# Copying the expert gate and up weights into 16 KB runs per partition during attention

## The chip, the cores and the metric

The kernel runs on one core of a Trainium2 chip (trn2). The metric is the device time of one execution in microseconds; the kernel before has a median of 1999.08 us in 3 runs, from 1995.08 to 2000.13 us. Everything is computed in 32-bit floats. The engines are named as in the profile: PE (TensorE, the matmuls), PEld (its weight loads), DVE (VectorE), ACT (ScalarE), POOL (GpSimd) and SP (SyncE, which here only issues DMAs). SBUF is the memory on the core with 128 partitions, PSUM takes the matmul results, and DRAM is the memory outside.

## The reference

One layer of a streaming encoder over 2048 tokens of width 1024:

```
h = modulate(rms_norm(x), sh1, sc1);  proj = h @ w_in
attn = latent attention (8 heads, chunks of 64 tokens, block-causal)
conv = gated depthwise convolution of 3 taps
x = x + g1 * (concat(rms_norm(attn), rms_norm(conv)) @ w_out)
h2 = modulate(rms_norm(x), sh2, sc2)
x = x + g2 * hier_moe(h2)        # top group of 4, then top 2 of its 8 experts
return rms_norm(x, final_g)
```

The part that the change feeds is the mixture of experts. Each of the 32 experts is a small MLP, `(silu(h @ w_gate[e]) * (h @ w_up[e])) @ w_down[e]`, with `w_gate` and `w_up` of shape 32 x 1024 x 256 and `w_down` of 32 x 256 x 1024. So an expert has 1 MB each of gate, up and down weights, 96 MB in all.

## The kernel before

The program has six stages, each a function with a block of its own in which every engine has a list of work. A stage begins when all engines have left the one before. In the profiled execution they lie roughly so: `project` (0 to 440 us) computes the modulation and the input projection; `attend` (443 to 1060 us) the attention; `mix` (1060 to 1330 us) the output projection and the router's logits; `route` and the tables at the start of `experts` choose tokens (to 1378 us); `experts` runs to 1950 us; `combine` does the last norm.

**Attention.** PE, DVE, ACT and POOL work through 8 heads, in two Python-unrolled halves `b` inside 4 values of `hp` (a loop on SP, unrolled on the others). A head has 40 steps (`STEPS_HEAD`), and its queries go in 4 groups of 512 (`GROUPS`). When a group is complete, ACT copies the sums out of PSUM, DVE inverts them and POOL multiplies (`divide`, line 1207) into one of the two buffers `on`, and counts up `divided`. SP waits for that count and stores `on` to `mix_dram` with two DMAs of 64 KB (line 802), counting `stored[0]` or `stored[1]`. POOL's `divide` two groups later reuses the buffer and first waits for that store (`hold(po, stored[p], ...)`). The last thing that SP does in the stage is to wait until all stores have landed. In this stage SP issues nothing else but two small loads of constants at its start.

**Mixing.** Its first DMAs, issued by SP as soon as the block begins, are a tile of `mix_dram` (line 1300), `w_out` in 4 parts of 1 MB (line 1314), the late modulation sums (1297) and a tile of `x` (1303). ACT issues the router's weights (lines 1522 to 1527). ACT and DVE then split `w_out` into a high and a low part (1562, 1509) before PE can begin (1347).

**Experts.** A loop over 16 pairs of experts. For each expert `b` of a pair, POOL gathers up to 192 token rows from `xs_dram` by an indirect DMA (`xa`, `xb`, line 1792), PE turns them (1863, 1864, 1874), ACT and DVE copy them to `xTe`. `gate_up` multiplies them by the gate and up weights (PE, line 1886), ACT and DVE make the activation, `down_first` and `down_rest` multiply by the down weights (1894), and POOL adds the scaled result to `x2_dram` by an indirect, accumulating DMA (1796). The weights have two buffers each, `wg`, `wu` and `wd`, one for each expert of a pair. SP waits for `up_done`, which PE raises when it is through with the buffers, and issues the next gate and up loads (lines 1782, 1783), then waits for `dlo_ready` and issues the down load (1785). In DRAM a gate or up matrix is 1024 rows of 256 numbers, so that each piece of such a load is 1 KB; each partition takes 8 of them. PE waits for both with one count, 32 for an expert (`ld_gu`).

Of the kernel before, what the change touches and what calls it, by code (L numbers as in the profile page):

```python
# [8 lines left out]
P = 128  # L9
# [8 lines left out]
D = 1024  # L18
KD = D // P
S = 2048  # L20
# [16 lines left out]
NEXP = 32  # L37
NGRP = 4
EPG = NEXP // NGRP
FE = 256  # L40
KF = FE // P
CAP = 192
# [642 lines left out]
GROUPS = NT // GQ  # L685
# [38 lines left out]
def attend(nc, T, st):  # L724
# [5 lines left out]
    with ExitStack() as ctx:  # L730
        sb = lambda name, shape, dt=F32: ctx.enter_context(nc.sbuf_tensor(name, shape, dt))
        sem = lambda name: ctx.enter_context(nc.semaphore(name))
        cst, cols, cs, qn, kvn, KR, mix_dram = (st[k] for k in (
            "cst", "cols", "cs", "qn", "kvn", "KR", "mix_dram"))
        Qhi, Qlo = sb("Qhi", [P, 2, S], F32R), sb("Qlo", [P, 2, S], F32R)
        Khi, Klo = sb("Khi", [P, 2, S], F32R), sb("Klo", [P, 2, S], F32R)

# [22 lines left out]
        scores_done, out_done, out_free, divided = (sem(n) for n in (  # L760
            "scores_done", "out_done", "out_free", "divided"))
        stored = [sem("on_stored0"), sem("on_stored1")]
        dve_step, inverted, passed_pool = sem("dve_step2"), sem("inverted"), st["passed_pool"]
        block = ctx.enter_context(nc.Block())

        def key_cols(i, n):

            return min(512, (i + 1) * P - n * 512)
# [17 lines left out]
        @block.sync  # L786
        def _(sp):
            for k in range(2):
                sp.dma_start(qf[QKD:QKD + 1 + GQ, k], T["consts"][QKD:QKD + 1 + GQ, C_ROWS + k * 512:C_ROWS + (k + 1) * 512]
                             ).then_inc(ld_rows, 16)  # L790
            sp.sem_inc(stored[0], 32)
            sp.sem_inc(divided, 2)
            sp.sem_inc(plo_done, RING)

            for s in st["done_sems"]:
                sp.sem_clear(s)
            with sp.Fori(0, HEADS // 2) as hp:
                for b in range(2):
                    for g in range(GROUPS):
                        sp.wait_ge(divided, hp * 2 * GROUPS + (b * GROUPS + g + 4))  # L800
                        for h in range(2):
                            sp.dma_start(mix_dram[VD * b:VD * (b + 1), bass.ds(hp, 1),
                                                  g * 512 + h * 256:g * 512 + (h + 1) * 256],
                                         on[h * VD:(h + 1) * VD, (g + 1) % 2:(g + 1) % 2 + 1]
                                         ).then_inc(stored[(g + 1) % 2], 16)
            sp.wait_ge(stored[0], 32 * (HEADS * GROUPS // 2 + 1))
            sp.wait_ge(stored[1], 32 * HEADS * GROUPS // 2)

# [913 lines left out]
def experts(nc, T, st):  # L1722

    with ExitStack() as ctx:
        sb = lambda name, shape, dt=F32: ctx.enter_context(nc.sbuf_tensor(name, shape, dt))
        sem = lambda name: ctx.enter_context(nc.semaphore(name))
        cst, modc, rank, marks, rounds, xs_dram, x2_dram, g2row = (st[k] for k in (
            "cst", "modc", "rank", "marks", "rounds", "xs_dram", "x2_dram", "g2row"))
        PAIRS = NEXP // 2
        inslot = sb("inslot", [P, NT * 2, CAP], BF16)  # L1730

# [9 lines left out]

        xT = sb("xTe", [P, KD, 2 * CAP])
        cols_of = (slice(0, CAP), slice(CAP, 2 * CAP))
        wg, wu, wd = sb("wg", [P, 2, KD, FE]), sb("wu", [P, 2, KD, FE]), sb("wd", [P, 2, KF, D])
        sg, aT = sb("sg", [P, KF, CAP]), sb("aT", [P, KF, CAP])

        dhi, dlo = sb("dhi", [P, 2, KF, D], F32R), sb("dlo", [P, 2, KF, D], F32R)
# [3 lines left out]
        turn, gate, up, outa, outb = bank[:, 0:2], bank[:, 2], bank[:, 3], bank[:, 4:6], bank[0:CAPB, 6:8]  # L1751
# [5 lines left out]
        ld_gu, ld_wd = [sem("ld_gu0"), sem("ld_gu1")], [sem("ld_wd0"), sem("ld_wd1")]  # L1757
        gate_done, up_done, silu_done = sem("gate_done"), sem("up_done"), sem("silu_done5")
# [9 lines left out]
        def load_rounds(eng):  # L1768
            return eng.value_load(rounds[0:1, 0:1], min_val=1, max_val=ROUNDS)

        @block.sync
        def _(sp):
            n_rounds = load_rounds(sp)
            wgd = T["w_exp_gate"].rearrange("l e (k p) n -> p (l e k) n", p=P)
            wud = T["w_exp_up"].rearrange("l e (k p) n -> p (l e k) n", p=P)
            wdd = T["w_exp_down"].rearrange("l e (k p) n -> p (l e k) n", p=P)
            with sp.Fori(0, n_rounds) as r:
                with sp.Fori(0, PAIRS) as ep:
                    for b in range(2):

                        sp.wait_ge(up_done, r * NEXP + ep * 2 + (b + 1))
                        sp.dma_start(wg[:, b], wgd[:, bass.ds(ep * 2 * KD + b * KD, KD), :]).then_inc(ld_gu[b], 16)
                        sp.dma_start(wu[:, b], wud[:, bass.ds(ep * 2 * KD + b * KD, KD), :]).then_inc(ld_gu[b], 16)
                        sp.wait_ge(dlo_ready, r * NEXP + ep * 2 + (b + 1))
                        sp.dma_start(wd[:, b], wdd[:, bass.ds(ep * 2 * KF + b * KF, KF), :]).then_inc(ld_wd[b], 16)

# [62 lines left out]
        def _(pe):  # L1849
# [26 lines left out]

            def gate_up(q, b, r):

                pe.wait_ge(ld_gu[b], r * (PAIRS * 32) + q * 32 + 32)
                pe.wait_ge(turn_dve, r * (PAIRS * 3) + q * 3 + (3 + b))  # L1880
                pe.wait_ge(turn_act, r * (PAIRS * 3) + q * 3 + (3 + b))
                pe.wait_ge(mlp_step, r * (NEXP * 3) + q * 6 + (b * 3 + 1))
                for w, out, done in ((wg, gate, gate_done), (wu, up, up_done)):
                    for f in range(KF):
                        for k in range(KD):
                            ins = pe.matmul(out[:, f * CAP:(f + 1) * CAP], w[:, b, k, f * P:(f + 1) * P],  # L1886
                                            xT[:, k, cols_of[b]], start=k == 0, stop=k == KD - 1)
                    ins.then_inc(done, 1)

# [21 lines left out]
            with pe.Fori(0, n_rounds) as r:  # L1911
# [4 lines left out]
                for first, last, b, lo, at in ((0, P, 4, 0, tokens), (0, CAPB, 5, P, tokens), (CAPB, P, 5, P, tokens),  # L1916
                                               (0, P, 6, 0, others), (0, CAPB, 7, P, others)):
                    pe.wait_ge(slots_ready, r * 2 + (1 if b == 4 else 2))
                    for j in range(NT * 2):
                        ins = pe.matmul(bank[first:last, b, at], inslot[:, j, lo:lo + last - first],  # L1920
                                        marks[:, j // 2, j % 2, at], start=j == 0, stop=j == NT * 2 - 1)
# [267 lines left out]
def program(nc, T, out):  # L2189
    with ExitStack() as whole:  # L2190
        def tensor(scope, side=None):
            return lambda name, shape, dt=F32: scope.enter_context(nc.sbuf_tensor(name, shape, dt, side=side))

        keep = tensor(whole)
        scratch = lambda name, shape: nc.dram_tensor(name, shape, F32, kind="Internal").ap()
        st = {"done_sems": [], "cst": keep("cst", [P, C_SMALL]), "cols": keep("cols", [P, 96]), "modc": keep("modcol", [P, 32]),
              "csil": keep("csil", [P, KD]),
              "mod_dram": scratch("mod_dram", [P, LATE_HALVES, 512]), "g1row": keep("g1row", [P, D]), "g2row": keep("g2row", [P, D]), "fgrow": keep("fgrow", [P, D]),
              "mix_dram": scratch("mix_dram", [P, 2 * NCH, S]), "x2_dram": scratch("x2_dram", [S + 2 * CAP, D]),
              "xs_dram": scratch("xs_dram", [S, D])}  # L2200

        st["passed"], st["passed_pool"] = (whole.enter_context(nc.semaphore(n)) for n in ("passed", "passed_pool"))
        with ExitStack() as mixers:
            left = tensor(mixers)
            st["cs"] = left("cs", [P, S])
            st["wuq"] = left("wuq", [P, KQ, (HEADS + 1) * QKD])
            st["wuk"], st["wuv"] = left("wuk", [P, (HEADS + 1) * NOPE]), left("wuv", [P, (HEADS + 2) * VD])
            st["qn"], st["kvn"], st["KR"] = left("qn", [P, KQ, S]), left("kvn", [P, S]), left("KR", [P, S])
            project(nc, T, st)
            attend(nc, T, st)  # L2210
        st["logits"] = keep("logits", [P, NT, NGRP + NEXP])
        mix(nc, T, st)
        st["gates"], st["rank"] = keep("gates", [P, NT * 2]), keep("rank", [P, NT * 2])
        st["marks"], st["rounds"] = keep("marks", [P, NT, 2, MARKS * NEXP], BF16), keep("rounds", [P, 1], I32)
        route(nc, T, st)
        experts(nc, T, st)
        combine(nc, T, st, out)
# [20 lines left out]
```

## Time and profile before

| | us |
|---|---|
| median of 3 runs | 1999.08 |
| lowest and highest run | 1995.08, 2000.13 |
| span of the profiled execution | 1996.9 |
| PE busy in the span | 1804.3 (90%) |
| DVE, ACT, POOL busy | 1181.1, 854.9, 855.0 |
| bytes read from and written to DRAM | 229.13 MB, 60.82 MB |

The profile has one profiled execution. Its page gives busy times, the span in 40 slices of about 50 us (a digit is a busy share in tenths; 9 is 90% or more), the DMA queues, the costliest groups of instructions and the DMA issues. Behind the page stands the trace, which can be asked for windows of time, for waits and who ended them, and for the instructions in order. The DMA share is the mean over the core's 16 DMA engines; as packets overlap it can pass 1. PE's granted clock is given as a share of full speed. "Landing" is the time from the issue of a DMA to the arrival of its last byte.

### The profile page before, as it was taken

The page shows a single profiled execution, that of the slowest core. Times are in us where ns is not written, and L with a number is a line of the kernel's source. Part 1 is how long each engine was busy: PE and PEld are TensorE (multiplying, and loading weights), DVE is VectorE, ACT ScalarE, POOL GpSimd, SP SyncE. Part 2 cuts the span into 40 slices and gives each one's busy share as a digit, 9 for nine tenths or more (in the row PEclk, how much of TensorE's full clock was granted, in tenths as well). Part 3 has the DMA queues.
Part 4 walks back from the last instruction along what each step waited for, and adds up shares of the span by engine and source line. Part 5 has one row for each costly group of instructions (what it writes and reads, how often), then busy time and mean ns, then how long its engine had stood idle before and what let it go on. Part 6 is the DMA issues. An engine that isn't in the chain of part 4 may idle for free. (4 is left out here: it accounts for less than half of the span.)

```text
span 1996.9 us, 26921 instructions
## 1 busy us (share of the span) xinstructions
PE 1804.3 (90%) x8987; PEld 1482.5 (74%) x8988; DVE 1181.1 (59%) x2015; ACT 854.9 (43%) x1520; POOL 855.0 (43%) x887
## 2 busy tenths in 40 slices
PE   2999999997999999999995999965999999999970
PEld 2777878764777777777784788854999988888960
DVE  4687889956766766666645555553444444444434
ACT  3535454326777677667684132311222222222214
POOL 0132314103888888888892111122243434434330
PEclk9999999996999999999996999977999999999995
DMA  7656555530000000000006344415899998999948
GB/s 282 197 164 185 172 163 165 147 95 0 6 9 6 9 9 6 11 7 6 11 11 218 105 157 141 143 43 189 278 268 276 279 276 270 278 276 274 272 91 336
DMA packets 216176, 291.05 MB, mean 146 GB/s; under 512 B 24373, under 2 KB 172048, under 8 KB 215834
## 3 DMA queue, kind: packets, MB, share of 16 engines
q1 hardware_dynamic: 193498, 220.60, 33.3%
q0 software_dynamic: 20224, 69.22, 13.9%
q8 instruction: 43, 0.70, 0.1%
q10 hardware_dynamic: 2368, 0.17, 0.1%
q14 instruction: 43, 0.35, 0.1%
HBM read 229.13 MB, written 60.82 MB: 145 GB/s over the span
## 5 line engine op out<-in xcount | busy, mean ns | idle before, releaser
L1212 POOL TENSOR_TENSOR plo<-KR,phi 128x512 fp32r<-128x512 f32 (+1 forms) x320 | 352.3, 1118 | 44.8 <-ACT KR L1171 44.6
L1020 DVE TENSOR_REDUCE cmax<-tbank 128x1 f32<-128x512 f32 (+2 forms) x320 | 193.4, 605 | 106.4 <-PE tbank L835 101.2
L1170 ACT ACTIVATE phi<-tbank 128x512 fp32r<-128x512 f32 (+1 forms) x320 | 170.7, 533 | 141.6 <-PE tbank L884 137.1
L387 PE MATMUL pbank<-hhi,wslhi 128*128 128x512 f32 x512 | 207.9, 406 | 6.7 <-DVE wsllo L440 6.7
L1946 DVE TENSOR_SCALAR xTe<-ebank,modcol 128x256 f32<-128x256 f32 (+1 forms) x128 | 53.7, 472 | 258.9 <-PE ebank L1864 137.6
L387 PE MATMUL pbank<-hhi,wsllo 128*128 128x512 f32 x512 | 201.9, 394 | 0.0
L387 PE MATMUL pbank<-hlo,wslhi 128*128 128x512 f32 x512 | 201.9, 394 | 0.0
L331 POOL DMA_DIRECT2D wmod<-in_w_ada x64 | 48.4, 757 | 305.2 <-DVE macc L519 295.2
L1886 PE MATMUL ebank<-xTe,wg 128*128 128x192 f32 x1024 | 171.8, 326 | 3.1 <-DVE ahi L1974 1.8
L1886 PEld LDWEIGHTS ebank<-xTe,wg 128*128 128x128 f32 x1024 | 167.9, 190 | 7.9 <-DVE ahi L1974 2.1
L1886 PE MATMUL ebank<-xTe,wu 128*128 128x192 f32 x1024 | 171.6, 326 | 0.0
L1171 ACT ACTIVATE KR<-tbank 128x512 f32<-128x512 f32 (+1 forms) x320 | 169.2, 529 | 0.0
L1886 PEld LDWEIGHTS ebank<-xTe,wu 128*128 128x128 f32 x1024 | 167.3, 190 | 0.0
L2080 ACT ACTIVATE xTe<-ebank,modcol 128x256 f32<-128x256 f32 (+1 forms) x128 | 56.7, 508 | 233.9 <-PE ebank L1864 147.1
L925 PE MATMUL tbank<-phi,VVhi 128*128 128x512 f32 (+1 forms) x320 | 134.7, 421 | 3.8 <-ACT phi L1170 3.7
L835 PE MATMUL tbank<-Khi,Qhi 96*128 96x512 f32 (+2 forms) x320 | 122.0, 384 | 5.4 <-DVE cmax L1020 5.1
L1573 POOL TENSOR_TENSOR mlo<-mixed,mhi 128x1024 fp32r<-128x1024 f32 x16 | 38.3, 2394 | 200.9 <-ACT mhi L1533 200.9
L387 PEld LDWEIGHTS pbank<-hhi,wslhi 128*128 128x128 f32 x512 | 97.7, 191 | 30.0 <-DVE wsllo L440 7.8
L883 PE MATMUL tbank<-Qhi,Klo 96*128 96x512 f32 (+1 forms) x320 | 118.2, 370 | 0.0
L903 PE MATMUL tbank<-plo,VVhi 128*128 128x512 f32 (+1 forms) x322 | 117.8, 366 | 0.3 <-POOL plo L1212 0.2
L884 PE MATMUL tbank<-Qlo,Khi 96*128 96x512 f32 (+1 forms) x320 | 117.9, 368 | 0.0
L926 PE MATMUL tbank<-phi,VVlo 128*128 128x512 f32 (+1 forms) x320 | 117.3, 367 | 0.0
(283 smaller groups left out, 3976.8 us busy)
## 6 DMA issues: line engine op xcount, KB each, us to landing
wg<-in_w_exp_gate SPq DMA_DIRECT2D x32, 1024.0 KB, 5.9
wu<-in_w_exp_up SPq DMA_DIRECT2D x32, 1024.0 KB, 9.0
wd<-in_w_exp_down SPq DMA_DIRECT2D x32, 1024.0 KB, 7.6
wraw<-in_w_in SPq DMA_DIRECT2D x60, 512.0 KB, 4.2
wmod<-in_w_ada POOLq DMA_DIRECT2D x64, 256.0 KB, 3.4
xt<-in_x SPq DMA_DIRECT2D x4, 2048.0 KB, 12.7
wada<-in_w_ada SPq DMA_DIRECT2D x4, 2048.0 KB, 18.7
mixed<-mix_dram SPq DMA_DIRECT2D x16, 512.0 KB, 4.3
```

The source lines that it names most:

```text
L387: ins = pe.matmul(out, w[:, S % 3, k], h[:, n % 2, k], start=k == 0 and j == 0, stop=k == KD - 1 and j == 2)
L835: pe.matmul(plain[:, chunk % 2, 0:w], Qhi[0:QKD, b, i * P:(i + 1) * P], Khi[0:QKD, b, n * 512:n * 512 + w], start=True, stop=True).then_in ...
L883: pe.matmul(out, Klo[0:QKD, b, k], Qhi[0:QKD, b, q], start=False, stop=False)
L884: pe.matmul(out, Khi[0:QKD, b, k], Qlo[0:QKD, b, q], start=False, stop=True).then_inc(scores_done, 1)
L903: ins = pe.matmul(outp[:, g % 2, first_tile(g, kt) * P:512], heads_values(VVhi, kt, b), step_of(plo, m), start=False, stop=last)
L925: pe.matmul(out, heads_values(VVhi, kt, b), step_of(phi, m), start=kt == 0, stop=False)
L926: pe.matmul(out, heads_values(VVlo, kt, b), step_of(phi, m), start=False, stop=False)
L1020: W(ve.tensor_reduce(cmax[:, i % 2, n:n + 1], plain[:, chunk % 2, 0:w], AX.X, ALU.max), plain_read)
L1170: A(act.activation(step_of(phi, m), scores[:, m % 2, j * P:512], ACT.Exp), phi_done)
L1171: A(act.activation(step_of(probs, m), scores[:, m % 2, j * P:512], ACT.Exp), exp_done)
L1212: po.tensor_tensor(step_of(plo, m), step_of(probs, m), step_of(phi, m).bitcast(F32), ALU.subtract).then_inc(plo_done, 1)
L1886: ins = pe.matmul(out[:, f * CAP:(f + 1) * CAP], w[:, b, k, f * P:(f + 1) * P], xT[:, k, cols_of[b]], start=k == 0, stop=k == KD - 1)
```

## The change

A new scratch tensor in DRAM, `wgu_dram`, holds for each expert and partition one run of 16 KB: 8 KB of gate weights and then 8 KB of up weights, in the order in which the partition takes them. During attention, each time that SP has issued the two stores of a group, it issues two copies of 1 MB from `w_exp_gate` and `w_exp_up` to `wgu_dram`, DRAM to DRAM, for one expert (`copy_expert`). With 8 heads of 4 groups that makes the 32 experts. At the end of the stage SP waits until all 64 copies have landed, ahead of its waits for the stores. In the experts, the buffers `wg` and `wu` become one, `wgu`, of the same size; one DMA of 2 MB takes the place of the two of 1 MB, and PE waits for 16 in place of 32.

```diff
+            def copy_expert(hp, j):
+                for n, name in enumerate(("w_exp_gate", "w_exp_up")):
+                    src = T[name].rearrange("l e (k p) n -> p (l e k) n", p=P)
+                    sp.dma_start(wgu_rows[:, bass.ds(hp * 2 * GROUPS + j, 1), n * KD:(n + 1) * KD],
+                                 src[:, bass.ds(hp * 2 * GROUPS * KD + j * KD, KD)].rearrange(
+                                     "p (e k) n -> p e k n", e=1)).then_inc(expert_copied, 16)
+
             with sp.Fori(0, HEADS // 2) as hp:
                 for b in range(2):
                     for g in range(GROUPS):
...
                                          ).then_inc(stored[(g + 1) % 2], 16)
+                        copy_expert(hp, b * GROUPS + g)
+            sp.wait_ge(expert_copied, 16 * 2 * NEXP)
             sp.wait_ge(stored[0], 32 * (HEADS * GROUPS // 2 + 1))
...
-        wg, wu, wd = sb("wg", [P, 2, KD, FE]), sb("wu", [P, 2, KD, FE]), sb("wd", [P, 2, KF, D])
+        wgu, wd = sb("wgu", [P, 2, 2 * KD, FE]), sb("wd", [P, 2, KF, D])
...
-            wgd = T["w_exp_gate"].rearrange("l e (k p) n -> p (l e k) n", p=P)
-            wud = T["w_exp_up"].rearrange("l e (k p) n -> p (l e k) n", p=P)
+            wgud = wgu_dram.rearrange("(e p) k n -> p e (k n)", p=P)
...
-                        sp.dma_start(wg[:, b], wgd[:, bass.ds(ep * 2 * KD + b * KD, KD), :]).then_inc(ld_gu[b], 16)
-                        sp.dma_start(wu[:, b], wud[:, bass.ds(ep * 2 * KD + b * KD, KD), :]).then_inc(ld_gu[b], 16)
+                        sp.dma_start(wgu[:, b:b + 1].rearrange("p e k n -> p e (k n)"), wgud[:, bass.ds(ep * 2 + b, 1)]
+                                     ).then_inc(ld_gu[b], 16)
...
-                pe.wait_ge(ld_gu[b], r * (PAIRS * 32) + q * 32 + 32)
+                pe.wait_ge(ld_gu[b], r * (PAIRS * 16) + q * 16 + 16)
...
-                for w, out, done in ((wg, gate, gate_done), (wu, up, up_done)):
+                for lo, out, done in ((0, gate, gate_done), (KD, up, up_done)):
...
-                            ins = pe.matmul(out[:, f * CAP:(f + 1) * CAP], w[:, b, k, f * P:(f + 1) * P],
+                            ins = pe.matmul(out[:, f * CAP:(f + 1) * CAP], wgu[:, b, lo + k, f * P:(f + 1) * P],
```

## Rows read from the trace of the kernel before

**Rows 1.** Page: busy us, 40 slices in tenths, matmul groups (busy us, mean ns | idle)

```profile
PE 1804.3 (90%) x8987; PEld 1482.5 (74%) x8988; DVE 1181.1 (59%) x2015; ACT 854.9 (43%) x1520; POOL 855.0 (43%) x887
...
PE   2999999997999999999995999965999999999970
...
DMA  7656555530000000000006344415899998999948
...
L1886 PE MATMUL ebank<-xTe,wg 128*128 128x192 f32 x1024 | 171.8, 326 | 3.1 <-DVE ahi L1974 1.8
...
L1886 PE MATMUL ebank<-xTe,wu 128*128 128x192 f32 x1024 | 171.6, 326 | 0.0
```

**Rows 2.** Windows by stage: length, busy per engine (instructions), PE clock, DMA share, GB/s

```profile
400.00:1050.00 650.00, 628.16 (x2755) 472.87 (x2754) 409.85 (x862) 436.68 (x909) 486.79 (x515) 0.97 0.05 14
...
1350.00:1950.00 600.00, 563.14 (x3360) 507.62 (x3360) 261.75 (x349) 132.64 (x194) 220.37 (x227) 0.97 0.86 252
```

**Rows 3.** The same view, one pair of experts of the loop

```profile
1657.00:1692.00 35.00, 35.00 (x205) 31.66 (x204) 16.09 (x21) 8.13 (x12) 14.54 (x16) 1.00 0.94 271
```

**Rows 4.** Waits in the experts: engine, line <- releaser: total us, times, longest

```profile
PE ebank L1863 <- DMA xb<-xs_dram,ib: 9.3, 1, 9.3
```

**Rows 5.** Waits of the SP queue in the experts, same columns

```profile
SPq L1782 <- PE ebank L1886: 203.2, 30, 28.2
```

**Rows 6.** DMA issues by line: count, KB each, median us to landing

```profile
wg<-in_w_exp_gate SPq DMA_DIRECT2D x32, 1024.0 KB, 5.9
wu<-in_w_exp_up SPq DMA_DIRECT2D x32, 1024.0 KB, 9.0
...
mix_dram<-on SPq DMA_DIRECT2D x64, 64.0 KB, 1.9
```

**Rows 7.** Timeline where attention ends: start us, length us, engine, operation [idle before]

```profile
1057.64 1.13 SPq L802 DMA_DIRECT2D mix_dram<-on  x2
1060.65 0.66 SPq L1300 DMA_DIRECT2D mixed<-mix_dram  x1
...
1060.65 0.46 ACTq L1522 DMA_DIRECT2D wr<-in_w_router_group  x1
...
1071.92 1.19 PE L1347 MATMUL mbank<-whi,mhi 128*128 128x512 f32 x2 [18.72 <-DVE wlo L1509]
```

**Rows 8.** Timeline of POOL: the divides that release the stores

```profile
521.78 0.73 POOL L1207 TENSOR_TENSOR on<-raw,rs 128x256 f32<-128x256 f32 x1
...
1013.03 0.74 POOL L1207 TENSOR_TENSOR on<-raw,rs 128x256 f32<-128x256 f32 x1
...
1030.69 0.74 POOL L1207 TENSOR_TENSOR on<-raw,rs 128x256 f32<-128x256 f32 x1
...
1045.01 0.74 POOL L1207 TENSOR_TENSOR on<-raw,rs 128x256 f32<-128x256 f32 x1
...
1056.76 0.72 POOL L1207 TENSOR_TENSOR on<-raw,rs 128x256 f32<-128x256 f32 x1 [3.94 <-DVE rs L1037]
```

**Rows 9.** Windows: first expert weights; last scatters (1942:1946); final stage

```profile
1358.00:1362.00 4.00, 2.17 (x37) 2.02 (x38) 3.84 (x3) 0.00 (x0) 0.00 (x0) 0.50 1.09 361
1362.00:1366.00 4.00, 4.00 (x78) 3.94 (x76) 1.09 (x6) 0.00 (x0) 0.00 (x0) 0.59 1.05 388
...
1942.00:1944.00 2.00, 0.00 (x0) 0.00 (x0) 0.00 (x0) 0.00 (x0) 0.20 (x1) 0.50 0.98 180
1944.00:1946.00 2.00, 0.00 (x0) 0.00 (x0) 0.00 (x0) 0.00 (x0) 0.00 (x0) 0.50 0.83 160
...
1965.00:1970.00 5.00, 0.00 (x0) 0.00 (x0) 2.01 (x6) 3.29 (x8) 0.00 (x0) 0.50 1.03 410
```

**Rows 10.** Timeline at the experts' start, and landing of the xb gathers

```profile
1368.92 0.96 POOL L1792 DMA_INDIRECT xb<-xs_dram,ib  x1 [0.30 <-issue]
...
1378.32 0.47 PE L1863 MATMUL ebank<-cst,xa 128*128 128x128 f32 x1 [9.30 <-DMA xb<-xs_dram,ib]
...
DMA to landing us min/median/max: 5.0/5.4/9.2
```

More of the change, by code:

```diff
@@ L732, in attend @@
         sem = lambda name: ctx.enter_context(nc.semaphore(name))
-        cst, cols, cs, qn, kvn, KR, mix_dram = (st[k] for k in (
-            "cst", "cols", "cs", "qn", "kvn", "KR", "mix_dram"))
+        cst, cols, cs, qn, kvn, KR, mix_dram, wgu_dram = (st[k] for k in (
+            "cst", "cols", "cs", "qn", "kvn", "KR", "mix_dram", "wgu_dram"))
         Qhi, Qlo = sb("Qhi", [P, 2, S], F32R), sb("Qlo", [P, 2, S], F32R)
@@ L762, in attend @@
         stored = [sem("on_stored0"), sem("on_stored1")]
+        expert_copied = sem("expert_copied")
         dve_step, inverted, passed_pool = sem("dve_step2"), sem("inverted"), st["passed_pool"]
         block = ctx.enter_context(nc.Block())
+        wgu_rows = wgu_dram.rearrange("(e p) k n -> p e k n", p=P)
         def key_cols(i, n):
@@ L1726, in experts @@
         sem = lambda name: ctx.enter_context(nc.semaphore(name))
-        cst, modc, rank, marks, rounds, xs_dram, x2_dram, g2row = (st[k] for k in (
-            "cst", "modc", "rank", "marks", "rounds", "xs_dram", "x2_dram", "g2row"))
+        cst, modc, rank, marks, rounds, xs_dram, x2_dram, g2row, wgu_dram = (st[k] for k in (
+            "cst", "modc", "rank", "marks", "rounds", "xs_dram", "x2_dram", "g2row", "wgu_dram"))
         PAIRS = NEXP // 2
@@ L2199, in program @@
               "mix_dram": scratch("mix_dram", [P, 2 * NCH, S]), "x2_dram": scratch("x2_dram", [S + 2 * CAP, D]),
-              "xs_dram": scratch("xs_dram", [S, D])}
+              "xs_dram": scratch("xs_dram", [S, D]),
+              "wgu_dram": scratch("wgu_dram", [NEXP * P, 2 * KD, FE])}
         st["passed"], st["passed_pool"] = (whole.enter_context(nc.semaphore(n)) for n in ("passed", "passed_pool"))
```

## The prediction, made before the changed kernel was run

> **What bounds the kernel now.** I read the page first. TensorE (PE) is busy for 90% of the span, and the PE line of the 40 slices stays at 9 except where one stage hands over to the next; the DMA line is at 8 or 9 over the last third, the experts, and at 0 over the attention [rows 1]. Those two lines invite the change, so the question is whether the busy DMA engines of the experts hold anything up. The table of windows by stage says how much there could be: attention (400 to 1050 us) has DMA at 0.05, the experts (1350 to 1950 us) have DMA at 0.86 and PE 563.14 of 600 us [rows 2]. The 36.86 us without PE are not in the loop: a window of about one pair of experts, 35 us, has PE busy for 35.00 us at clock 1.00, with DMA at 0.94 beside it [rows 3]. The waits of that stage agree. Only one wait of PE on a DMA is there, 9.3 us, once, for the first gathered rows [rows 4]. None is for wg or wu. The wait runs the other way: the SP queue, which issues the weights, stood 203.2 us in 30 waits for PE to free a buffer [rows 5]. A 1 MB weight transfer lands in 5.9 us (gate) or 9.0 us (up, queued behind it) [rows 6]. Its buffer is free for a pair's 35 us less the gate and up matmuls of one expert, (171.8 + 171.6) / 32 = 10.7 us [rows 1]: 24 us. So the loop is bound by PE and the weights are hidden, with 15 us to spare.
>
> The other place that matters is the end of attention, where the new work ends. The last two stores are issued from 1057.64 us, 1.13 us for both; the mixing stage's first DMAs start at 1060.65 us on the SP and ACT queues at the same instant, so a barrier lets them go, and it waits for the store to land, 1.9 us [rows 6, 7]. From there to the first matmul of the mixing stage at 1071.92 us everything is a chain of loads and splits with no cover: PE stood for 18.72 us [rows 7].
>
> **The change, part by part.** *Expert loads.* Two 1 MB issues per expert become one of 2 MB, with 16 KB runs. In the loop it removes waits of nobody. Even if it took 2 or 3 us off each landing, PE would still have 0 us to win; if 16 KB runs were somehow slower, the 15 us of slack cover that. I enter 0; it would cost from a landing above 24 us on. The SP queue issues one DMA less per expert, 32 in all, at about 0.5 us; SP waits for PE anyway [rows 5], so 0.
>
> *Start of the experts.* Here loads and gathers do meet. The gather of xb is issued at 1368.92 us and PE starts on it at 1378.32 us, 9.4 us later, while its landings have a median of 5.4 us [rows 10]. It is behind what is left of the first 6.3 MB of weights. The engines move these at 361 and 388 GB/s with 1 KB gate and up rows; the last stage, all rows of 4 KB, reaches 410 [rows 9]. If 16 KB runs brought the 4.2 MB of gate and up from 375 to 410 GB/s, they would end 11.2 - 10.2 = 1.0 us sooner. Bounds: 0 and, if the gather were wholly freed, 9.4 - 5.4 = 4.0 us. I take 0.5 us gained, since the other transfers stay.
>
> *The copies in attention.* 32 pairs of 1 MB copies, DRAM to DRAM, 1 KB pieces, 67.1 MB. They touch no SBUF, and the engines of attention wait for no loads. The DMA share there is 0.05 [rows 2], so the room is there. Each pair is issued on SP behind the two stores of a group. The store that follows is queued behind it, and POOL's divide, two groups later, waits for that store. Where divides come closest, in the last head, two of them span 1030.69 - 1013.03 = 17.7 us [rows 8]; a store behind one pair is in time as long as T + 1.9 is less than that. That part is 0.
>
> *The last copy.* This is the term that counts. The last pair is issued right behind the last store, and the new wait on expert_copied stands ahead of the barrier. Queued behind that wait are all DMAs of the mixing stage, and all five engines. Nothing hides it. Its cost is one issue between the last store and the first copy (0.5 us, about half of the 1.13 us [rows 7]) plus the transfer time T of 2.10 MB; the fixed 1.9 us to land is paid already by the store.
>
> T has no row: no transfer of the kernel before goes from DRAM to DRAM. Above, a copy cannot beat a plain load or store, 410 GB/s in the last stage where both directions mix [rows 9]: T = 5.1 us. The nearest row from below is the accumulating scatter, which reads DRAM and writes it back within one packet: with nothing else in flight it moved 180 and 160 GB/s (counted once) at engine shares 0.98 and 0.83 [rows 9], so 184 to 193 GB/s at full share: T = 11.4 us. If an engine's read and write side share the 410 GB/s of the mixed row, a copy gets 205 GB/s: T = 10.2 us; with the loss of 1 KB rows (375 against 410) it is 187 GB/s and T = 11.2 us. These last three agree and I take 190 GB/s, T = 11.0 us.
>
> The Trainium skill (DMA: Bandwidth & Descriptors, Latency and other measured facts) gives 207 to 214 GB/s per direction for copies between HBM tensors with 16 KiB rows and slower ones where the pitch between partitions is 512 KiB or more; here it is 16 KB and 1 KB. By it T would be an estimated 10.0 us and the sum 1 us lower; no row of before shows such a copy.
>
> *Backlog.* Is the queue empty when the last pair is issued? The last five divides are at 1013.03 us, one between, 1030.69, 1045.01 and 1056.76 us [rows 8], each sending one pair some 2 us later (1056.76 us for the last, its stores from 1057.64 us and 1.13 us long), so the five have moved by 1015 + 5T or by 1058.8 + T, whichever is later, and land 1.9 us behind. The two cross at T = 11.0 us. So at 11.0 there is no backlog yet, but no margin either: each us of T beyond it costs 5 us. In the earlier heads a pair has 18.2 us on average: the divide at 1013.03 us is the 27th after the one at 521.78 us, which lets the first pair go [rows 8].
>
> **The sum.** 0.5 + 11.0 - 0.5 = +11.0 us on the profiled execution: span 1996.9 to 2007.9 us. The median of the runs, 1999.08 us, stands 2.2 us above the span, as start and end outside it; so 2010.1 us.
>
> **Rivals.** (1) *Backlog*: the copy runs at 140 to 170 GB/s, because each 1 KB piece costs the engines more between two DRAM addresses than the scatter's 4 KB pieces. T = 13.5 us: the five pairs end at 1015 + 67.5 + 1.9 = 1084.4 instead of 1060.3 us, +24 us, less 0.5: 2022.7. For it speaks that the scatter's row was taken with 4 KB pieces; against it that loads with 1 KB pieces lose only 9%. It decides from T = 11.0 us.
> (2) *Fast copy*: read and write overlap fully, T = 5.1 to 7 us, +5.6 to +7.5, less 0.5: 2005. The scatter speaks against it, though its addition may be what slows it.
> (3) *Not slower*: the same fast copy, +5.6 us, and the first gather finds an empty queue, -4.0 us: 2000.7. With the whole 4.0 us gained, it decides from T below 9.5 us (0.5 + 9.5 - 4.0 = 6.0 us, 0.3%). Against it: the DMA engines are full at 1.09 and 1.05 while the first weights load [rows 9], so bytes, not runs, set the end. For a time well below 1999 I find no idle time of PE that the change could remove beyond the 9.3 us [rows 4].
> (4) *Copies that don't fit*: below 115 GB/s (2.1 MB in 18.2 us) the queue grows through all of attention. At 100 GB/s, T = 21: 523 + 32 x 21 = 1195 us instead of 1060, +135 us: 2134. The stores would also hold POOL's divides. Nothing in the trace points so low.
>
> **How the numbers follow.** Forecast (T of 9 to 11.5 us, 2008 to 2013) 0.52; backlog 0.24; fast copy 0.12; not slower 0.07; doesn't fit 0.05. A measurement of this kernel can tell about 0.3% (6 us) from no change, 1993.1 to 2005.1. The fast copy straddles the bound with half of its chance, so same gets 0.06 + 0.06 = 0.12; faster 0.03, from a gain at the start of the experts that I have no row for; slower 0.85. The range leaves out part of rival 3 below and rival 4 and the slow end of rival 1 above: 2003 to 2028.
>
> **What would show it.** In the profile after: DMA share in attention about 0.6 (11.0 of 18.2 us) where it was 0.05; PE in attention unchanged at 628 us of 650; the first DMA of the mixing stage 11 us later behind the last store, and PE's wait before its first matmul near 30 us where it was 18.72; the expert loop still about 35 us a pair with PE full, whatever the landing of wgu. The landing of the copies tells T: with the second of a pair above some 13 us the backlog is there. Wrong would be: a wait of PE or POOL in attention on a store or on its own instructions, a pair of experts that gets shorter, or a handover that is not longer than before.

## The result

The changed kernel takes 2005.21 us (median of 10 runs, 2001.75 to 2007.38), the kernel before 1998.83 us in the same series (10 runs). The medians differ by 6.4 us, 0.32%. The ratio on record, which is not the quotient of these two medians, is 1.0039, with a 95% interval from 1.0027 to 1.0050: slower by 5.4 to 10.0 us. The profiled execution has a span of 2002.6 us where it was 1996.9 us, +5.7. The forecast was 2010.1 us, +11.0.

The page after the change: span, busy times, PE and DMA over the 40 slices, and the DMA issues that are new (count, KB each, median us to landing).

```profile
span 2002.6 us, 27098 instructions
...
PE 1802.1 (90%) x8988; PEld 1479.4 (74%) x8988; DVE 1181.2 (59%) x2015; ACT 855.3 (43%) x1520; POOL 858.2 (43%) x887
...
PE   2899999997999999999994999965999999999970
...
DMA  7656555520233442432547344414889889989848
...
wgu<-wgu_dram SPq DMA_DIRECT2D x32, 2048.0 KB, 8.5
wgu_dram<-in_w_exp_gate SPq DMA_DIRECT2D x32, 1024.0 KB, 6.1
wgu_dram<-in_w_exp_up SPq DMA_DIRECT2D x32, 1024.0 KB, 7.5
```

PE and the other engines are as busy as before [rows 1]. Where the DMA line stood at 0 during attention it now has 2 to 5, and the largest part of the longer span is the handover to the mixing stage, as shown below. The windows by stage (length, busy time per engine with instructions, PE clock, DMA share, GB/s):

```profile
400.00:1050.00 650.00, 627.94 (x2742) 472.00 (x2741) 409.31 (x861) 435.17 (x905) 484.74 (x512) 0.97 0.34 110
...
1350.00:1950.00 600.00, 568.29 (x3392) 511.18 (x3390) 267.61 (x361) 132.99 (x195) 228.86 (x231) 0.97 0.82 251
```

In attention PE is busy for 627.94 us of 650, before 628.16, with the DMA engines at 0.34 instead of 0.05 [rows 2]. In the experts the DMA share fell from 0.86 to 0.82 at the same 251 GB/s, with the same bytes in longer runs, and PE is as busy as it was in the loop (the window of the table is fixed, and the stage now begins later in it).

The end of attention is the place. The timeline of the SP queue there, and PE's first matmul of the mixing stage (start us, length us):

```profile
1059.75 1.24 SPq L812 DMA_DIRECT2D mix_dram<-on  x2
1061.28 0.64 SPq L803 DMA_DIRECT2D wgu_dram<-in_w_exp_gate  x1
1062.18 0.64 SPq L803 DMA_DIRECT2D wgu_dram<-in_w_exp_up  x1
1069.99 0.64 SPq L1312 DMA_DIRECT2D mixed<-mix_dram  x1
...
1081.36 1.19 PE L1359 MATMUL mbank<-whi,mhi 128*128 128x512 f32 x2 [26.07 <-DVE wlo L1521]
```

The stretch from the issue of the last stores to the first load of the next stage is called the handover below. It took 1060.65 - 1057.64 = 3.0 us [rows 7] and takes 1069.99 - 1059.75 = 10.2 us: +7.2. Of these 10.2 us, 1.5 pass until the first copy is issued and 0.9 more until the second, which on the median lands 7.5 us later. PE's idle time before its first matmul there grew from 18.72 us [rows 7] to 26.07 us: +7.35. That is about the whole loss, 6.4 us by the medians and 7.8 by the ratio.

### The profile page after: what moved, and what is told of

The parts are those of the page before. It is cut to its first block and busy times, and to the rows that moved or that the text cites. A ratio compares the mean times of both kernels' runs of the same rounds, so it can differ in the third digit from the quotient of the medians.

```text
span 2002.6 us, 27098 instructions
## 1 busy us (share of the span) xinstructions
PE 1802.1 (90%) x8988; PEld 1479.4 (74%) x8988; DVE 1181.2 (59%) x2015; ACT 855.3 (43%) x1520; POOL 858.2 (43%) x887
## 5 line engine op out<-in xcount | busy, mean ns | idle before, releaser
L1897 PE MATMUL ebank<-xTe,wgu 128*128 128x192 f32 x2048 | 339.6, 327 | 3.1 <-DVE ahi L1985 1.8
L1897 PEld LDWEIGHTS ebank<-xTe,wgu 128*128 128x128 f32 x2048 | 335.7, 191 | 7.9 <-DVE ahi L1985 2.1
L894 PE MATMUL tbank<-Qhi,Khi 97*128 97x512 f32 (+2 forms) x320 | 117.7, 368 | 0.0
L387 PEld LDWEIGHTS pbank<-hhi,wsllo 128*128 128x128 f32 x512 | 96.8, 189 | 20.9
```

The source lines that it names most:

```text
L387: ins = pe.matmul(out, w[:, S % 3, k], h[:, n % 2, k], start=k == 0 and j == 0, stop=k == KD - 1 and j == 2)
L894: pe.matmul(out, Khi[0:every, b, k], Qhi[0:every, b, q], start=True, stop=False)
L1897: ins = pe.matmul(out[:, f * CAP:(f + 1) * CAP], wgu[:, b, lo + k, f * P:(f + 1) * P], xT[:, k, cols_of[b]], start=k == 0, stop=k == KD - 1)
```

## The ledger of one execution

The start times of the same events in both traces, in us (before, after, and what was added since the row above):

| event | before | after | added |
|---|---|---|---|
| first divide of attention | 509.67 | 511.36 | +1.7 |
| last divide | 1056.76 | 1058.85 | +0.4 |
| first load of the mixing stage | 1060.65 | 1069.99 | +7.3 |
| first matmul of the mixing stage | 1071.92 | 1081.36 | +0.1 |
| first expert load issued | 1354.73 | 1361.34 | -2.8 |
| first gathered rows turned | 1378.32 | 1382.83 | -2.1 |
| end of the span | 1996.9 | 2002.6 | +1.2 |

Two of these differences need a word. The first is there before any copy, and the -2.8 us of the mixing stage lie within what that stage varies by. The first divides of the two kernels, as POOL's timeline shows them:

```profile
509.67 0.73 POOL L1207 TENSOR_TENSOR on<-raw,rs 128x256 f32<-128x256 f32 x1
```

```profile
511.36 0.73 POOL L1219 TENSOR_TENSOR on<-raw,rs 128x256 f32<-128x256 f32 x1
...
1058.85 0.72 POOL L1219 TENSOR_TENSOR on<-raw,rs 128x256 f32<-128x256 f32 x1 [3.94 <-DVE rs L1049]
```

The first copy is issued at 526.9 us, so the 1.7 us that lie ahead of it can't come from copies. They go with PE's granted clock: in the windows of 3 us it is back at 1.00 from 493 us on before and from 499 us on after. Over all twelve profiles of this study, attention from PE's first matmul to the last divide takes either 612.9 to 613.4 us (eight, five of them with copies) or 616.0 to 616.6 us (four, all with copies, the changed kernel among them). The difference lies ahead of the first divide: from the first to the last divide all twelve take 547.1 to 547.5 us, the three without copies 547.1 or 547.2. So the copies cost attention at most 0.4 us behind its first divide, and in the changed kernel the rest is there before the first copy. The mixing stage, from its first matmul to the first expert load, takes 279.9 to 284.3 us; the loads-alone kernel below, which has no copies, takes 280.0 like the changed kernel, against 282.8 before. One profile of each kernel is therefore good to some 3 us, and the timed ratios decide. Of the -2.1 us at the start of the experts 1.7 are the shorter wait for the first gather, and the +1.2 us at the end go with a clock that rises late; both follow below.

## Experiments

All start from the changed kernel or, where it says so, from the kernel with early copies or the kernel before. The ratios are to the kernel before as it ran in the same series, with 95% intervals; its median was 1999.68 us in the series of the first four, 2000.76 us in that of the next four and 2001.55 us (one run) in the last.

### The copies one place earlier

```diff
                     for g in range(GROUPS):
+                        copy_expert(hp, b * GROUPS + g)
                         sp.wait_ge(divided, hp * 2 * GROUPS + (b * GROUPS + g + 4))
...
-                        copy_expert(hp, b * GROUPS + g)
```

> The changed kernel, but each pair of copies is issued ahead of SP's wait for the group's stores instead of behind the stores, so the last pair goes out about 12 us before the last store. Bytes, waits and expert loads are the same. Theory A (the loss is the last pair alone, exposed at the end of attention): SP's queue from last store to first load of the mixing stage falls from 10.2 us back to about 3.0 us, PE's wait before its first matmul from 26.1 to about 18.7 us, and the time to about 7.3 us below the changed kernel, 1998; that is 0.999 of the kernel before. Theory B (67 MB of copies slow attention itself, by contention or late instructions): the handover recovers but attention stays longer, and the time stays at 2003 to 2005, 1.003. Theory C (clock phases that fall by chance explain a good part): between the two.

Measured: 2000.3 us, ratio 1.0001 (0.9991 to 1.0011). The SP queue at the end of attention:

```profile
1047.08 1.23 SPq L813 DMA_DIRECT2D mix_dram<-on  x2
1048.59 0.64 SPq L803 DMA_DIRECT2D wgu_dram<-in_w_exp_gate  x1
1049.48 0.63 SPq L803 DMA_DIRECT2D wgu_dram<-in_w_exp_up  x1
1058.81 1.23 SPq L813 DMA_DIRECT2D mix_dram<-on  x2
1061.98 0.65 SPq L1312 DMA_DIRECT2D mixed<-mix_dram  x1
```

The last pair goes out at 1048.59 and 1049.48 us, 9.3 us ahead of the last store at 1058.81 us, and the next stage's first load follows that store by 3.2 us. PE's wait before the mixing stage is 18.89 us, 18.72 before:

```profile
1073.24 1.19 PE L1359 MATMUL mbank<-whi,mhi 128*128 128x512 f32 x2 [18.89 <-DVE wlo L1521]
```

Attention takes 613.1 us here with all 67 MB of copies in it, 613.3 us in the kernel before. The order of two issues is all that differs, so theory A holds: the loss is the exposure of the last pair. Theory B, copies that slow attention, falls. The time, 1.0001, is above the 0.999 that I expected: the gather's 1.8 us do not arrive in the end (below).

### The copies without their use

The edit is, without the two lines that name the inputs and the count of 32 that PE waits for again:

```diff
-                        sp.dma_start(wgu[:, b:b + 1].rearrange("p e k n -> p e (k n)"), wgud[:, bass.ds(ep * 2 + b, 1)]
-                                     ).then_inc(ld_gu[b], 16)
+                        sp.dma_start(wgu[:, b, 0:KD], wgd[:, bass.ds(ep * 2 * KD + b * KD, KD), :]).then_inc(ld_gu[b], 16)
+                        sp.dma_start(wgu[:, b, KD:], wud[:, bass.ds(ep * 2 * KD + b * KD, KD), :]).then_inc(ld_gu[b], 16)
```

> The copies and the wait of the change, but the experts load gate and up with two 1 MB transfers from the inputs, as before; what is copied is read by nobody. Theory A: handover +7.2 us as in the changed kernel, PE's wait for the first gathered rows back at 9.3 us instead of 7.6, ratio about 1.0036 to 1.004. If the 16 KB loads were worth more than the first gather (rival), this is slower than the changed kernel by more than 2 us, 1.005 or above.

Measured: 2007.33 us, ratio 1.0035 (1.0021 to 1.0049); the handover is 10.4 us. PE's wait for the first gathered rows (total us, times, longest) is the old one [rows 4]:

```profile
PE ebank L1875 <- DMA xb<-xs_dram,ib: 9.3, 1, 9.3
```

The copies alone cost what the change costs.

### The loads without the copies

```diff
-                        copy_expert(hp, b * GROUPS + g)
-            sp.wait_ge(expert_copied, 16 * 2 * NEXP)
...
-            wgud = wgu_dram.rearrange("(e p) k n -> p e (k n)", p=P)
+            wgud = [T[name].rearrange("l e (k p) n -> (l e k p) n", p=P).rearrange("(e p k) n -> p e (k n)", p=P, k=2 * KD)
+                    for name in ("w_exp_gate", "w_exp_up")]
...
-                        sp.dma_start(wgu[:, b:b + 1].rearrange("p e k n -> p e (k n)"), wgud[:, bass.ds(ep * 2 + b, 1)]
+                        sp.dma_start(wgu[:, b:b + 1].rearrange("p e k n -> p e (k n)"), wgud[b][:, bass.ds(ep, 1)]
```

> No copies and no wait for them; the experts load 2 MB in one transfer with 16 KB runs, but straight from the gate (even experts) and up (odd experts) inputs, read as if they were laid out so. The weights are thus the wrong ones, so what the experts compute is changed; bytes, instructions and token routing are not. It prices the load alone. Theory A: only the first gather gains, PE's wait there 7.6 instead of 9.3 us, time 1.7 us below before, 0.9991 (0.998 to 1.000); the loop keeps 35 us a pair with PE full. Rival (the loads matter in the loop): more than 5 us below before, 0.997 or less.

Measured: 1998.98 us, ratio 0.9997 (0.9986 to 1.0007). PE's wait for the first rows:

```profile
PE ebank L1873 <- DMA xb<-xs_dram,ib: 7.6, 1, 7.6
```

So the one thing that the change is for, 16 KB runs and one transfer of 2 MB, shortens that wait by 1.7 us and is worth nothing that the times can tell. It does relieve the DMA engines. The same window of the loop, first with the copies alone (1 KB pieces), then with the loads alone (16 KB runs), has PE full in both and a DMA share of 0.93 and 0.90 (ahead of the GB/s):

```profile
1600.00:1700.00 100.00, 100.00 (x586) 91.06 (x585) 44.38 (x58) 21.59 (x33) 40.33 (x39) 1.00 0.93 271
```

```profile
1600.00:1700.00 100.00, 100.00 (x587) 91.08 (x586) 44.12 (x57) 22.17 (x35) 40.84 (x39) 1.00 0.90 274
```

In the loop of the changed kernel PE is full, as it was [rows 3]:

```profile
1600.00:1700.00 100.00, 100.00 (x582) 89.97 (x581) 46.32 (x60) 23.92 (x35) 40.84 (x41) 1.00 0.90 276
```

### Where the gather's gain goes

The changed kernel at the start of the experts: the gather of xb is issued at 1375.21 us and PE begins 7.6 us later, 9.4 us before [rows 10].

```profile
1375.21 0.96 POOL L1803 DMA_INDIRECT xb<-xs_dram,ib  x1 [0.30 <-issue]
...
1382.83 0.47 PE L1874 MATMUL ebank<-cst,xa 128*128 128x128 f32 x1 [7.60 <-DMA xb<-xs_dram,ib]
```

But from that first transposition to PE's last matmul the time is 1934.99 - 1378.32 = 556.7 us before and 1941.00 - 1382.83 = 558.2 us after: what the gather gave is taken back. The windows of 1.5 us behind it show by what, first of before and then of after (the column ahead of the last two is PE's granted clock):

```profile
1379.80:1381.30 1.50, 1.26 (x7) 0.80 (x5) 0.67 (x2) 0.98 (x2) 0.00 (x0) 0.50 0.00 0
1381.30:1382.80 1.50, 1.20 (x6) 0.72 (x4) 1.00 (x2) 0.31 (x2) 0.13 (x2) 0.65 0.01 5
1382.80:1384.30 1.50, 0.51 (x3) 0.52 (x4) 0.00 (x0) 0.75 (x2) 0.69 (x3) 1.00 0.00 0
```

```profile
1387.30:1388.80 1.50, 0.48 (x2) 0.49 (x3) 0.00 (x0) 0.78 (x2) 0.69 (x3) 0.50 0.00 0
...
1390.30:1391.80 1.50, 1.50 (x7) 1.50 (x7) 0.00 (x0) 0.00 (x0) 0.22 (x1) 0.65 0.78 273
1391.80:1393.30 1.50, 1.50 (x11) 1.50 (x10) 0.00 (x0) 0.00 (x0) 0.00 (x0) 1.00 0.92 243
```

In the kernel before the clock rose from 0.50 to 1.00 (1.2 to 2.4 GHz) about 4 us after PE had started again, in the changed kernel about 8.5 us after. The first gate and up matmuls then run at half speed, up to 684 ns each where the mean is 326. The twelve profiles fall into the same two kinds. In four of them the full clock is back 3.6 to 4.0 us after the restart: with a wait of 9.3 us (two kernels), where the rest takes 556.6 and 556.7 us, and with 5.8 and 6.1 us (two kernels, next section), where it takes 556.5 us. In the other eight it is back only after 8.5 to 11.6 us: with waits of 7.0 to 7.6 us (six kernels), where the rest takes 558.2 to 558.9 us, and with 8.6 and 10.7 us in the two kernels of the last experiment. So both shorter and longer waits than 7.6 us have met an early clock, and the longest wait of all a late one: the length of the wait does not settle it. What does was not tested.

### The gather ahead of the second expert's weights

Both the kernel with early copies and the kernel before got one wait more on SP, for the landing of xb. In the loop it is met long before; it acts only at the start:

```diff
                         sp.wait_ge(up_done, r * NEXP + ep * 2 + (b + 1))
+                        if b:
+                            sp.wait_ge(gathered_b, r * (PAIRS * 16) + ep * 16 + 16)
```

> As the kernel with the copies ahead of the stores, and SP also waits for the first gather of each pair before it loads the second expert's weights; in the loop that gather is long past, so only the start changes: 3 MB instead of 6.3 MB are in front of the first gathers. Theory A (the first gathers are queued behind weights): PE's wait for the first rows falls from 7.6 to about 4.5 us, and the time another 3 us, to 1995, 0.998 of before. Rival (the gather's 5 us are its own latency and the queue adds little): no change against the kernel with the copies ahead.

Measured: 1996.94 us, ratio 0.9987 (0.9976 to 0.9997), PE's wait:

```profile
PE ebank L1876 <- DMA xb<-xs_dram,ib: 5.8, 1, 5.8
```

> The kernel before, without any copy, with one wait added on SP: ahead of the second expert's gate load it waits until that pair's first gather has landed. It asks whether the gain of the version with both edits (0.9987) needs the 16 KB runs at all. Theory: the time of the first gather is set by the bytes in front of it, 3.1 MB instead of 6.3, so PE's wait there falls from 9.3 us to about 6 us, and the ratio is the same 0.9987 (0.998 to 0.9995). Rival (it needs the faster copied loads): PE's wait stays at 9 us, ratio 1.000.

Measured: 1997.1 us, ratio 0.9984 (0.9975 to 0.9993), PE's wait:

```profile
PE ebank L1865 <- DMA xb<-xs_dram,ib: 6.1, 1, 6.1
```

Expected were 4.5 and 6 us for the wait, 5.8 and 6.1 came. Both are a little faster than the kernel before, and equal to each other within their intervals: the order of issue gives 3 us (1.4 to 5.0 in the second kernel), and it needs none of the copies. What is left of the wait, 5.8 and 6.1 us, is near the 5.4 us that a gather of xb takes to land anywhere in the loop [rows 10]. And here the clock rose early, so that nothing of the shorter wait was lost again. Of all kernels tried these two are the fastest; the second is the kernel before with one line.

### The wait moved to the experts

The edit, without the lines that make the semaphore one of the whole program:

```diff
-            sp.wait_ge(expert_copied, 16 * 2 * NEXP)
             sp.wait_ge(stored[0], 32 * (HEADS * GROUPS // 2 + 1))
...
+            sp.wait_ge(st["expert_copied"], 16 * 2 * NEXP)
             with sp.Fori(0, n_rounds) as r:
```

> The changed kernel, but the wait for the copies stands at the start of the experts instead of the end of attention; the order of issue is as in the change. So the barrier no longer waits for the last pair, whose 2.1 MB now lie in the DMA queue ahead of the mixing stage's first loads. Theory A (bytes ahead in the queue cost what the wait cost): the handover falls from 10.2 to 3.1 us, but PE's wait before its first matmul of the mixing stage only from 26.1 to about 24 us, and the time stays 5 us over before, 1.0025. Theory B (the wait itself is the cost, the queue has room): PE's wait falls to about 19 us, ratio 1.000.

Measured: 2002.64 us, ratio 1.0012 (1.0003 to 1.0021).

```profile
1060.00 0.64 SPq L803 DMA_DIRECT2D wgu_dram<-in_w_exp_up  x1
1061.33 0.69 SPq L1311 DMA_DIRECT2D mixed<-mix_dram  x1
1062.06 3.51 SPq L1325 DMA_DIRECT2D wout<-in_w_out  x2
...
1077.67 1.19 PE L1358 MATMUL mbank<-whi,mhi 128*128 128x512 f32 x2 [24.55 <-DVE wlo L1520]
```

The barrier now lets go early, 3.8 us behind the issue of the stores, and the first load leaves at 1061.33 us. PE still waits for 24.55 us, 5.8 more than before, because the copies' 2.1 MB are ahead of the first loads. So in PE's idle time the wait is the small part (1.5 us) and the bytes in front of a stage that lives on its loads are the large one (5.8 us). The times do not bear this split out. Theory A named 24 us and a ratio of 1.0025; the idle time agrees, but the ratio is 2.4 us over before (0.6 to 4.2) where the change itself was 5.4 to 10.0 over. Taken by the ratios, moving the wait gives back more than half of the loss; but the two kernels were timed in different series, and their intervals are wide. This profile had a mixing stage of 279.9 us, 2.9 shorter than before, but so had the changed kernel (280.0), so that does not explain it. Where the rest comes back is left open.

### The price of a pair

```diff
-            sp.wait_ge(expert_copied, 16 * 2 * NEXP)
+            spare = st["spare"].rearrange("(e p) k n -> p e k n", p=P)
+            for j in range(2):
+                for n, name in enumerate(("w_exp_gate", "w_exp_up")):
+                    src = T[name].rearrange("l e (k p) n -> p (l e k) n", p=P)
+                    sp.dma_start(spare[:, j:j + 1, n * KD:(n + 1) * KD],
+                                 src[:, j * KD:(j + 1) * KD].rearrange("p (e k) n -> p e k n", e=1)
+                                 ).then_inc(expert_copied, 16)
+            sp.wait_ge(expert_copied, 16 * (2 * NEXP + 4))
```

That is the kernel with 1 KB pieces. The one with 8 KB pieces reads the source in another order, and both have the tensor `spare` besides (not shown).

> The changed kernel with two more pairs of such copies (4.2 MB, 1 KB pieces) to a spare tensor behind the last pair, ahead of the wait. It prices a pair by itself, apart from issue and landing. At the 387 GB/s seen at the end of attention in the changed kernel: 10.2 + 2 x 5.4 = 21.1 us between last store and first load. At the 190 GB/s of the prediction: 10.2 + 22 = 32 us.

> The same 4.2 MB more, but in 8 KB pieces (the source is read in the order in which it lies, so the spare tensor gets another order; nobody reads it). If the pieces of 1 KB cost nothing in a DRAM to DRAM copy, 21 us as with 1 KB pieces. If 1 KB pieces lose what they lose in loads (375 against 430 GB/s), about 1.3 us less, 19.8 us.

Measured: a handover of 24.9 us with 1 KB pieces (2020.52 us, one run) and of 24.0 us with 8 KB pieces (2020.33 us). Windows of 2 us of the first:

```profile
1064.00:1066.00 2.00, 0.00 (x0) 0.00 (x0) 0.00 (x0) 0.00 (x0) 0.00 (x0) 0.50 1.09 374
...
1070.00:1072.00 2.00, 0.00 (x0) 0.00 (x0) 0.00 (x0) 0.00 (x0) 0.00 (x0) 0.50 1.07 331
...
1074.00:1076.00 2.00, 0.00 (x0) 0.00 (x0) 0.00 (x0) 0.00 (x0) 0.00 (x0) 0.50 1.00 264
...
1078.00:1080.00 2.00, 0.00 (x0) 0.00 (x0) 0.00 (x0) 0.00 (x0) 0.00 (x0) 0.50 1.03 357
```

Against 10.2 us with one pair, a further pair costs (24.9 - 10.2) / 2 = 7.3 us, 287 GB/s over all, with 1 KB pieces and (24.0 - 10.2) / 2 = 6.9 us with 8 KB. That is neither of the two figures expected (5.4 and 11 us). The window from 1064 us, with the first pair under way, moves 374 GB/s; from 1066 to 1080 us it is 264 to 357 with the engines full or nearly so (share 0.91 to 1.09), and in the last 4 us they run empty (232 and 24 GB/s). The size of the pieces is not the main reason: 8 KB change 0.4 us a pair. Why a later pair moves more slowly was not tested.

### How full the DMA engines of the loop are

Copies of more bytes, 0.5 or 2 MB per expert, between the gate and up load and the down load, on top of the kernel with early copies (for 2 MB over both inputs, with 8 in place of 4; a wait for all of them at the end of the stage is not shown):

```diff
+                        for n, src in enumerate((gsrc, usrc)[:1]):
+                            sp.dma_start(spare[:, bass.ds(ep * 2 + b, 1), n * KD:n * KD + 4],
+                                         src[:, bass.ds(ep * 2 * KD + b * KD, 4)].rearrange(
+                                             "p (e k) n -> p e k n", e=1)).then_inc(more, 16)
```

> The kernel with the copies ahead of the stores, and 0.5 MB more per expert copied from DRAM to a spare tensor in the experts' loop, issued behind the gate and up load and ahead of the down load. It asks how much room the DMA engines have in the loop. A pair holds them for 0.94 x 35 = 32.9 us; 1.05 MB more at 387 GB/s and share 1.09 makes 35.9 us, which is under 35 x 1.09 = 38. Prediction's theory (PE bound, weights hidden with 15 us to spare): the loop stays at 35 us a pair, the weights land some 1.4 us later, the time within 2 us of the kernel without it, 2000. Rival (the queue is as good as full at 0.94): about 1 us or more per pair, 16 us in all.

> The same with 2 MB more per expert. The engines would be held for 32.9 + 11.8 = 44.7 us a pair, more than 38: the loop should turn DMA bound at about 44.7 / 1.09 = 41 us a pair, some 90 us more in all (2090), with PE waiting for wgu or ACT for wd. If PE stays full, the DMA share of the profile overstates what is used.

Measured: 2003.62 us and 2065.46 us, one run each. Windows of 100 us in the loop, first with 0.5 MB, then with 2 MB more:

```profile
1600.00:1700.00 100.00, 100.00 (x581) 89.97 (x580) 46.62 (x60) 23.90 (x35) 40.44 (x41) 1.00 0.97 306
```

```profile
1600.00:1700.00 100.00, 91.17 (x497) 81.75 (x496) 38.58 (x50) 19.64 (x31) 35.88 (x37) 0.95 1.03 343
```

With 0.5 MB more PE stays full and the loop, from the first transposition to PE's last matmul, is 559.7 us against 558.5: +1.2, where the rival named 16. The span is 3.3 us longer than with early copies alone, more than the 2 us expected; 2.3 of these lie ahead of the first divide. With 2 MB more it is 2001.6 - 1379.4 = 622.2 us, +64, and now PE and ACT wait for weights (total us, times, longest):

```profile
PE ebank L1906 <- DMA wgu<-wgu_dram: 43.9, 12, 5.9
...
ACT dhi L2118 <- DMA wd<-in_w_exp_down: 17.6, 6, 3.4
```

The engines reach a share of 1.03 and 343 GB/s, and the loop takes about 39 us a pair, where I had reckoned 41, and 64 us more in all, where I had reckoned 90. So a share of 0.94 was not the limit: the weights were hidden with room for at least 1.05 MB more a pair.

## Why the prediction was right, and which term was off

The forecast (+11.0 us, slower) had the right sign, place and mechanism, and its range held the time. It held it low down: 2005.21 us is outside the 2008 to 2013 us that I thought likeliest (0.52) and only 0.1 us above the bound of 2005.1 us up to which I would have called it no change. The single terms:

- *The loop gains nothing.* Right. PE is full in every window of the loop shown, with either kind of load; the loads alone give 0.9997; 1 MB more a pair does not make PE wait, 4 MB do.
- *Attention pays nothing for the copies.* Right: 613.1 us with early copies against 613.3 before, and at most 0.4 us from first to last divide in any kernel. The DMA share is 0.34 where I forecast 0.6, for the reason that follows.
- *The last pair is exposed, issue plus T.* Right in kind: +7.2 us of handover, and it goes to +0.2 when the pair leaves one group earlier. PE's wait before the mixing stage was forecast near 30 us and is 26.07.
- *T = 11.0 us.* This is the step that failed: the term was sized 4.3 us too large. I took 190 GB/s, from the accumulating scatter and from the thought that reading and writing share 410 GB/s. Windows of 1 us of the changed kernel show the pair itself:

```profile
1060.00:1061.00 1.00, 0.00 (x0) 0.00 (x0) 0.00 (x0) 0.00 (x0) 0.00 (x0) 0.50 0.03 9
...
1062.00:1063.00 1.00, 0.00 (x0) 0.00 (x0) 0.00 (x0) 0.00 (x0) 0.00 (x0) 0.50 0.28 58
1063.00:1064.00 1.00, 0.00 (x0) 0.00 (x0) 0.00 (x0) 0.00 (x0) 0.00 (x0) 0.50 0.78 189
1064.00:1065.00 1.00, 0.00 (x0) 0.00 (x0) 0.00 (x0) 0.00 (x0) 0.00 (x0) 0.50 1.09 387
...
1067.00:1068.00 1.00, 0.00 (x0) 0.00 (x0) 0.00 (x0) 0.00 (x0) 0.00 (x0) 0.50 1.08 386
1068.00:1069.00 1.00, 0.00 (x0) 0.00 (x0) 0.00 (x0) 0.00 (x0) 0.00 (x0) 0.50 0.93 330
```

  It moves at 330 to 387 GB/s, counted once, as fast as a load with 1 KB rows [rows 9] and twice as fast as the scatter. So reading and writing do not share the 410 GB/s. With 0.5 us of issue from the sum, the 7.2 us leave T = 6.7 us; this is a remainder and not a measurement by itself. The DMA share gives an estimate that does not need it: (0.34 - 0.05) x 650 us over the 30 pairs that move in that window are 6.3 us a pair. The lower bound of 5.1 us was sound and lay nearer. That is the second rival, the fast copy, which named 2005 for T from 5.1 to 7 us and to which I gave 0.12.
- *Backlog from T = 11.0 us.* It did not arise; T is well below. Each store in attention landed within 2.8 us.
- *The start of the experts, -0.5 us.* The wait shrank by 1.7 us, within the bounds of 0 and 4.0; 1.0 us sooner for the weights was reckoned at 410 GB/s, while with 16 KB runs two windows of 4 us at that place show 420 and 432 GB/s (361 and 388 before [rows 9]). But from the first expert load to PE's last matmul the two kernels need 580.3 and 579.7 us: -0.6. The small value was right by an effect, the late clock, that I had not seen.
- *The figure of the Trainium skill* (DMA: Bandwidth & Descriptors, Latency and other measured facts), 207 to 214 GB/s (the 207 is its value at a pitch of 512 KiB; only its larger pitches are much slower). It would have put T at an estimated 10.0 us, half as much again as the runs show; a first pair has 6.7 us, the pairs behind it 6.9 (8 KB pieces) and 7.3 us (1 KB). The measurement decides.

The sum with these terms is 0.5 + 6.7 - 0.6 = +6.6 us. As T is the remainder of the handover, this checks only that nothing else counts: the medians differ by 6.4 us, the two profiles by 5.7, and the interval runs from 5.4 to 10.0.

## What to carry to other kernels

A busy DMA line is no reason for faster transfers: ask first whether anybody waits for them, and where nobody does, prepare nothing for them. Work put into an idle stretch is free only if its last piece also ends there; the same copies cost 7 us behind the last store and nothing one group earlier. In front of a stage that begins with loads, bytes in the queue can hold up its first matmul nearly as long as a wait for them (5.8 against 7.35 us here), though in time the kernel with the wait moved lost less than that. And look at the order of issue first: one added wait on the kernel before, without any copy, was the better change.

## What the runs showed of the hardware

A single pair of 1 MB copies from DRAM to DRAM moved at up to 387 GB/s, counted once, with 1 KB pieces; three pairs in a row came down to 287 GB/s for the later two, and 8 KB pieces changed little. The same bytes in 16 KB runs into SBUF lowered the DMA share of the loop from 0.93 to 0.90, at 271 and 274 GB/s (copies alone and loads alone). A share above 0.9 left room: 1 MB more a pair of experts cost the loop 1.2 us in all, 4 MB more 64 us. And PE, restarting after a wait, got its full clock either 3.6 to 4.0 us after the restart (waits of 5.8, 6.1, 9.3 and 9.3 us) or 8.5 to 11.6 us after it (the eight others, 7.0 to 8.6 and 10.7 us); where a wait of 9.3 us became one of 7.6, the late clock swallowed the gain.
